# Contiguous first loads with two weight pieces in one pass, a reordered chain of expert choice, and the last row's norm on GpSimd

## What is computed

```python
x = layer_norm(DN_ALPHA * x + hybrid_mixer(x, ...), ln1_g, ln1_b)            # neighbourhood attention ++ short convolution
x = layer_norm(DN_ALPHA * x + memory_cross_attention(x, mem, ...), ln2_g, ln2_b)   # 4 heads over 256 memory rows
x = layer_norm(DN_ALPHA * x + expert_choice_moe(x, ...), ln3_g, ln3_b)

def expert_choice_moe(x, w_router, w_gate, w_up, w_down):                    # 16 experts, hidden width 2048
    affinity = softmax(x @ w_router)                                         # 512 x 16
    gates, idx = lax.top_k(affinity.T, 64)                                   # each expert takes its 64 best tokens
    hid = silu(x[idx] @ w_gate) * (x[idx] @ w_up)
    return scatter_add(idx, (hid @ w_down) * gates)
```

## Time and profile before

| | us |
|---|---|
| median of 3 runs | 1240.74 (1240.32 to 1240.86) |
| profiled execution | 1239.73 |
| its span | 1237.9 |
| PE busy | 1160.5 (94%) |
| DVE busy | 267.6 (22%) |
| ACT busy | 186.7 (15%) |
| POOL busy | 144.1 (12%) |
| chain that ended last | PE 71%, DMA 24%, DVE 2%, ACT 1% |
| HBM read | 440.99 MB |

### The profile page before, as it was taken

One profiled execution on the slowest core, in us unless ns is written; L12 is line 12 of the kernel. 1 busy time (PEld: TensorE's weight loads), 2 busy tenths in 40 slices (PEclk: granted clock), 3 DMA queues, 4 the chain that ended last, 5 costly groups with the idle time before them and its releaser, 6 DMA issues.

```text
span 1237.9 us, 13582 instructions
## 1 busy us (share of the span) xinstructions
PE 1160.5 (94%) x5770; PEld 587.0 (47%) x5770; DVE 267.6 (22%) x510; ACT 186.7 (15%) x341; POOL 144.1 (12%) x71
## 2 busy tenths in 40 slices
PE   8999999999999999999799979987998898899997
PEld 6887778888733433443243324332422342243432
DVE  3022457727700020010002000200010010002025
ACT  4244444143000000010000000000000010000100
POOL 4454334330000300000000000000000000000002
PEclk9999999999999999999999999999998999999999
DMA  9532223249799999999999999999999999999998
GB/s 371 185 135 77 74 94 134 80 186 422 303 338 426 428 423 429 432 431 430 433 428 431 432 432 431 430 434 428 434 431 433 427 436 430 434 426 428 427 427 334
DMA packets 30315, 443.92 MB, mean 359 GB/s; under 512 B 4738, under 2 KB 5122, under 8 KB 10692
## 3 DMA queue, kind: packets, MB, share of 16 engines
q1 hardware_dynamic: 27892, 440.85, 84.7%
q10 hardware_dynamic: 2304, 2.24, 0.5%
q0 software_dynamic: 80, 0.26, 0.1%
HBM read 440.99 MB, written 2.36 MB: 358 GB/s over the span
## 4 chain that ended last, share of the span: by engine, by line
PE 71%; DMA 24%; DVE 2%; ACT 1%; issue 1%; POOL 0%; POOLq 0%; SPq 0%; DVEq 0%; ACTq 0%
DMA ring<-in_w_exp 23%; PE bank L1322 22%; PE bank L1369 14%; PE bank L1196 5%; PE bank L1283 4%; PE bank L837 3%; PE bank L839 3%; PE bank L842 3%; PE bank L1021 1%; PE bank L1023 1%; PE bank L1022 1%; PE bank L1353 1%; PE bank L826 1%; DMA out<-xT 1%; PE bank L977 1%
## 5 line engine op out<-in xcount | busy, mean ns | idle before, releaser
L1322 PE MATMUL bank<-ring,yt 128*64 128x512 f32 x1952 | 440.8, 603 | 41.8 <-DMA ring<-in_w_exp 41.7
L1322 PEld LDWEIGHTS bank<-ring,yt 128*64 128x64 f32 x1952 | 144.0, 139 | 327.0 <-issue 266.8
L1369 PE MATMUL bank<-ring,yt 128*64 128x512 f32 x896 | 203.8, 608 | 20.1 <-DMA ring<-in_w_exp 14.6
L1369 PEld LDWEIGHTS bank<-ring,yt 128*64 128x64 f32 x896 | 64.7, 139 | 138.9 <-issue 123.9
L556 POOL TENSOR_TENSOR stat<-stat 128x1 f32<-128x1 f32 x12 | 18.4, 1530 | 756.7 <-DVE stat L1487 756.7
L1744 DVE TENSOR_TENSOR work<-bank,work 128x512 f32<-128x512 f32 x30 | 20.7, 691 | 355.3 <-PE bank L1322 355.3
L786 ACT ACTIVATE work<-bank 128x512 f32<-128x512 f32 x32 | 19.1, 597 | 478.6 <-PE bank L1322 478.6
L549 POOL TENSOR_TENSOR piece<-ring,piece 128x1024 fp32r<-128x1024 f32 x31 | 74.3, 2397 | 91.3 <-ACT piece L616 91.3
L1760 DVE TENSOR_TENSOR xT<-bank,xT 128x512 f32<-128x512 f32 x56 | 38.7, 692 | 137.1 <-PE bank L1283 137.1
L1196 PE MATMUL bank<-yt,res 128*128 128x128 f32 x512 | 60.0, 275 | 0.0
L1196 PEld LDWEIGHTS bank<-yt,res 128*128 128x128 f32 x512 | 58.4, 192 | 0.8 <-issue 0.8
(11 more groups left out here) (268 smaller groups left out, 1084.3 us busy)
## 6 DMA issues: line engine op xcount, KB each, us to landing
ring<-in_w_exp SPq DMA_DIRECT2D x55, 4096.0 KB, 29.9
ring<-in_w_exp SPq DMA_DIRECT2D x58, 2048.0 KB, 21.4
ring<-in_dense SPq DMA_DIRECT2D x12, 2048.0 KB, 7.8
ring<-in_w_exp SPq DMA_DIRECT2D x5, 3072.0 KB, 27.8
ring<-in_w_exp SPq DMA_DIRECT2D x11, 1024.0 KB, 29.4
spare<-in_w_exp SPq DMA_DIRECT2D x3, 2048.0 KB, 20.0
xT<-in_w_exp SPq DMA_DIRECT2D x4, 1024.0 KB, 9.4
ln<-in_w_exp SPq DMA_DIRECT2D x6, 512.0 KB, 12.8
```

The source lines that it names most:

```text
L1322: mm = nc.tensor.matmul(bank[2 * g + n % 2][64 * c:64 * c + 64, :], xeT[:, kk, 64 * e:64 * e + 64], exp_rhs(at + j, early, k, c), start=kk ...
L1369: mm = nc.tensor.matmul(bank[5][64 * n:64 * n + 64, :], hidT[:, s, 64 * c:64 * c + 64], exp_rhs(at + j, early, s, n), start=(g, c, s) == ( ...
```

## The change

Four things change.

1. The host lays x and the first two pieces of weights out as whole contiguous blocks. SP issues x in four parts with a quarter of pieces 0 and 1 behind each (eight loads instead of five up to there). ACT and POOL handle those quarters of both pieces (four each instead of two), and PE computes both pieces in one pass, with three fillers ahead and a short one in each of the first three steps.
2. DVE adds the two parts of the logits before the turning product (ACT did a copy), so four products and one DVE addition go. The copy of the transposed affinities out of PSUM goes: the rounds read PSUM. The gate copy goes behind the masks. The norm of token tile 3 (`gain` and `shift` on DVE, 128x1024 each) becomes three POOL instructions behind `inverse_std(7)`. The `shift` of token tile 2 is split in halves and put behind the rounds and behind the masks.
3. The rank products take float32r operands, whose constants ACT rounds ahead of the exponential. Two filler products stand behind the transposed masks; one instead of three stands behind the last round of the search.
4. The first gather takes two channel blocks into another bank, then two more; the first expert products start on the first two blocks, and the last four blocks are gathered in the middle of chunk 1 instead of one ahead of chunk 0 and three ahead of chunk 1. The one-hot matrix is made in two halves.

```diff
@@ SP
-            load_x(0)
-            load_first()
-            for m in range(1, KT // 2):
+            for m in range(KT // 2):
                 load_x(m)
-            for m in range(1, 4):
+                load_first(m)
+            for m in range(FIRST_PIECES, 4):
                 load_q(m)
@@ POOL, behind inverse_std(7)
+            row = res[:, TT - 1, :]
+            pool.wait_ge(rstd_ready, 2 * TT)
+            pool.wait_ge(ln_in, 32 * 2)
+            nc.gpsimd.tensor_scalar(row, row, mv_of(TT - 1)[:, 0:1], rstd(TT - 1), ALU.subtract, ALU.mult).then_inc(last_scaled, 1)
+            pool.wait_ge(last_scaled, 1)
+            nc.gpsimd.tensor_tensor(row, row, ln[:, 0, :], ALU.mult).then_inc(gained, 1)
+            pool.wait_ge(gained, 2 * TT)
+            nc.gpsimd.tensor_tensor(row, row, ln[:, 1, :], ALU.add).then_inc(normed, 1)
@@ ACT
-            act.wait_ge(o_logits_done, 1)
-            nc.scalar.activation(o_logits, ps[1][:, :], ACT.Copy).then_inc(o_logits_kept, 1)
+            act.wait_ge(late_in, 16)
+            for to, of in ((tri_r, cst[:, C_TRI:C_TRI + P]), (one_r, cst[:, C_ONE:C_ONE + P]),
+                           (upto_r, late_const(C_UPTO, P)), (below_r, late_const(C_BELOW, P))):
+                nc.scalar.activation(to[:, :], of, ACT.Copy).then_inc(tables_rounded, 1)
@@ PE, first_from_x
                 for k in range(KT):
-                    if k % 4 == 0:
-                        pe.wait_ge(first_hi, k // 4 + 1)
+                    if k % 2 == 0:
+                        pe.wait_ge(first_hi, k // 2 + 1)
                     pe.wait_ge(x_hi_kept, k + 1)
-                    nc.tensor.matmul(pj[0][:, :], hi[:, k, :], x_hi[:, k, :], start=k == 0, stop=False)
+                    for n in range(FIRST_PIECES):
+                        product(n, k, 0, x_hi)
+                    if k < 3:
+                        nc.tensor.matmul(px[0][:, 0:256], kv[:, 0:P], kv[:, 0:256], start=True, stop=True)
                     if k:
                         pe.wait_ge(x_lo_kept, k)
-                        nc.tensor.matmul(pj[0][:, :], hi[:, k - 1, :], x_lo[:, k - 1, :], start=False, stop=False)
+                        for n in range(FIRST_PIECES):
+                            product(n, k - 1, 0, x_lo)
+                    if k % 2 and k > 1:
+                        pe.wait_ge(first_lo, k // 2)
+                        for m in (k - 3, k - 2):
+                            product(0, m, 1, x_hi)
@@ PE, choice
-                keep_clock(3)
+                keep_clock(3 if r < CAP // 8 - 2 else 1)
...
+            keep_clock(2)
+            pe.wait_ge(tables_rounded, 4)
             pe.wait_ge(above_ready, 1)
             pe.wait_ge(turn_kept[TN_MASK % 2], TN_MASK // 2 + 1)
...
-            nc.tensor.matmul(ranks, cst[:, C_TRI:C_TRI + P], mask_tok, start=True, stop=False)
+            nc.tensor.matmul(ranks, tri_r[:, :], mask_r[:, :, :], start=True, stop=False)
@@ PE, pair
-                    gather(0, 4)
-                    gather(4, 5)
+                    gather(0, 2, to=pt, wait_halves=True)
+                    gather(2, 4)
...
-                            if j == 1 and first:
-                                gather(5, 8)
...
+                                if first and j == 1 and k == 2:
+                                    gather(4, 8)
@@ DVE
-            shift(res, 2, TT + 2)
-
-            lg = ps[0][:, 0:TT * E].rearrange("p (t e) -> p t e", t=TT)
+            dve.wait_ge(o_logits_done, 1)
+            for a in range(2):
+                at = slice(256 * a, 256 * a + 256)
+                nc.vector.scalar_tensor_tensor(o_logits[:, at], x1_logits[:, at], ALPHA, ps[1][:, at], ALU.mult, ALU.add)\
+                    .then_inc(o_logits_kept, 1)
...
-            nc.vector.tensor_copy(gate.rearrange("p i t e -> p t i e"), aff.rearrange("p t (i e) -> p t i e", e=2))\
-                .then_inc(gate_kept, 1)
-
-            gain(res, TT - 1, 2 * TT - 1)
             link(nc.vector.memset(lists[:, 0:1], 2.0))
             dve.wait_ge(turned, TN_AFF + 1)
-            nc.vector.tensor_copy(afft, pt[TN_AFF % 2][halves, 0:256]).then_inc(turn_kept[TN_AFF % 2], 1)
-            dve.wait_ge(turn_kept[TN_AFF % 2], TN_AFF // 2 + 1)
+            afft = pt[TN_AFF % 2][halves, 0:256]
...
+            shift_half(TT - 2, 0).then_inc(last_shifted, 1)
...
-            shift(res, TT - 1, 2 * TT - 1)
+            dve.wait_ge(last_shifted, 1)
+            shift_half(TT - 2, 1).then_inc(normed, 1)
+            nc.vector.tensor_copy(gate.rearrange("p i t e -> p t i e"), aff.rearrange("p t (i e) -> p t i e", e=2))\
+                .then_inc(gate_kept, 1)
```

More of the change, by code:

```diff
@@ L138 @@
 LAST_PARTS = {CPP - 2: 2, CPP - 1: 4}
-START_FILLERS = 2
+START_FILLERS = 3
+FIRST_PIECES = 2
+FIRST_LOADS = KT // 2
 def build(nc, x, x_turned, mem_turned, dense, na_bias, conv_w, ln1_g, ln1_b,
@@ L241, in build @@
         col_sums = stat[:, 64:96]
-        sum_groups = [cst[:, C_SUM + n * E:C_SUM + n * E + E] for n in range(2)]
+        sum_groups = cst[:, C_SUM:C_SUM + E]
         router_sums = stat[:, 64:96].rearrange("p (a e) -> p a e", a=2)
@@ L533, in _ @@
             nc.gpsimd.memset(neg_half, -0.5).then_inc(half_set, 1)
-            for a in range(2):
-                k = slice(4 * a, 4 * a + 4)
-                pool.wait_ge(first_hi, a + 1)
-                nc.gpsimd.tensor_tensor(piece[:, 0, 1, k, :], raw_piece(0)[:, k, :], piece[:, 0, 0, k, :].bitcast(F32),
+            for g in range(FIRST_LOADS):
+                pool.wait_ge(first_hi, g + 1)
+                nc.gpsimd.tensor_tensor(first_part(g, 1), first_raw(g), first_part(g, 0).bitcast(F32),
                                         ALU.subtract).then_inc(first_lo, 1)
@@ L629, in split_x, with split_first @@
                 nc.scalar.activation(x_hi[:, k, :], x_raw[:, k, :], ACT.Copy).then_inc(x_hi_kept, 1)
-            def split_first(a):
-                k = slice(4 * a, 4 * a + 4)
-                act.wait_ge(first_in, 16)
-                nc.scalar.activation(piece[:, 0, 0, k, :], raw_piece(0)[:, k, :], ACT.Copy).then_inc(first_hi, 1)
-            split_x(0)
-            split_first(0)
-            for k in range(1, 4):
-                split_x(k)
-            split_first(1)
-            for k in range(4, KT):
-                split_x(k)
-            split(1)
+            def split_first(g):
+                act.wait_ge(first_in[g], 16)
+                nc.scalar.activation(first_part(g, 0), first_raw(g), ACT.Copy).then_inc(first_hi, 1)
+            for g in range(FIRST_LOADS):
+                split_x(2 * g)
+                split_first(g)
+                split_x(2 * g + 1)
             nc.scalar.activation(edge_x[0].rearrange("p k (s t) -> p k s t", s=2), edge_tokens(x_raw), ACT.Copy)                .then_inc(edge_hi_kept, 1)
@@ L896, in _ @@
             first_from_x()
-            for p in range(1, 8):
+            for p in range(FIRST_PIECES, 8):
                 from_x(p)
@@ L1177, in _ @@
             keep_clock(5)
-            pe.wait_ge(chosen_ready, 1)
-            turn(TN_MASK, [(chosen[:, a, P * b:P * b + P], 2 * E, P) for a in range(2) for b in range(2)])
+            pe.wait_ge(turn_kept[TN_MASK % 2], TN_MASK // 2)
+            for a, ready in enumerate((gt_ready, chosen_ready)):
+                pe.wait_ge(ready, 1)
+                for b in range(2):
+                    at = P * (2 * a + b)
+                    mm = nc.tensor.transpose(pt[TN_MASK % 2][:, at:at + 2 * E], chosen[:, a, P * b:P * b + P], ident[halves, halves])
+            mm.then_inc(turned, 1)
+            keep_clock(2)
+            pe.wait_ge(tables_rounded, 4)
             pe.wait_ge(above_ready, 1)
@@ L1320, in pair @@
                                 kk = 4 * (n // 2) + k
+                                if first and j == 0 and k == 2:
+                                    pe.wait_ge(xe_kept, 1)
+                                if first and j == 1 and k == 2:
+                                    gather(4, 8)
                                 for c in range(2):
@@ L1839, in dense_chunks @@
               by_row(w_o), by_row(w_o.T)]
+    first, rest = chunks[0][:, 0:FIRST_PIECES], chunks[0][:, FIRST_PIECES:]
+    first = first.reshape(P, FIRST_PIECES, FIRST_LOADS, 2, P).transpose(2, 0, 1, 3, 4)
+    chunks[0] = np.concatenate([first.reshape(-1), rest.transpose(1, 0, 2, 3).reshape(-1)])
     return np.stack([c.reshape(P, SLOT) for c in chunks])
@@ L1860 @@
         "x": by_column(np.asarray(inputs["x"])[0]),
-        "x_turned": by_row(by_column(np.asarray(inputs["x"])[0]).T),
+        "x_turned": by_row(by_column(np.asarray(inputs["x"])[0]).T).reshape(P, KT // 2, 2, S).transpose(1, 0, 2, 3),
         "na_bias": bias_table(np.asarray(inputs["na_rpb"])[0]),
```

173 lines of the change are left out of this document (106 added, 67 removed).

## The result

The changed kernel takes 1234.39 us (median of 4 runs, 1233.03 to 1236.2), the kernel before 1240.8 beside it: a ratio of 0.9948, 95% interval 0.9935 to 0.996, some 6.4 us less. Two later sets of runs, on other chips, gave 5.6 and 5.4 us less. The prediction, 1243.7 with a range from 1235.8, had the wrong sign. What came was its first rival, "the chain gets shorter" (1236.1), and a little more. The profiled execution is the slowest of the four, 1236.2 us with a span of 1234.4, only 3.5 us under the span before: its work up to the last stores runs 4.65 us ahead, and these took 10.20 us where they had 9.08.

A forecast was written before the change was run, and what follows sets the result against it. It took the DMA plateau, started by pair 0, to bound the kernel. Start -1.3, softmax +6.1, behind it -0.9 and order in pair 0 -0.9 gave +3.0 on 1240.74: 1243.7 us, range 1235.8 to 1246.2.

The forecast's parts named there:

- first rival: Softmax: POOL's three instructions leave DVE's small steps alone, affinities 0.2 us earlier; 1236.1 us in all, chance 0.20.
- The frame: DMA queue: the end is the plateau's start plus fixed bytes, so moving pair 0's start moves the end equally.
- Nothing arrives: DMA queue: its backlog, not pair 0, sets the plateau, so no term counts; 1240.7 us, chance 0.05.
- Softmax, +6.1: Choice of experts: POOL's three instructions hold DVE's two-SBUF-operand softmax steps; +6.1 us (+3.9 to +6.8).
- That rival: Softmax: TENSOR_SCALAR does not block, only the division is caught, affinities +1.9 us; 1238.2 us, chance 0.08.
- Idle PE, low clock and piled-up fillers (+1.2): Behind the softmax: PE idles 6 us; slower transposes cost 0.2 us, fillers of the rounds +1.0 (0 to 2.0).
- MAX8 behind the affinities: Behind the softmax: without gate copy, gain and PSUM copy only the transpose is left, 0.6 us: -1.3.
- Ranks: Behind the softmax: eight float32r rank products take one pass each, 1.25 us in all: -0.85 (0 to -1.1).
- The half pick: Between ranks and gather: six fillers stand as before, so the earlier half of `pick` gains nothing.
- Order in pair 0: First expert pair: chunk 0 starts 0.9 us earlier and reloads move forward; -0.9 us (-1.2 to 0).
- Start, -1.3: Kernel start: the third piece starts near 19.75 instead of 21.05 us; -1.3 us (-2.0 to -0.1).
- the 0.8 for the clock: Kernel start: half-speed products before TensorE reaches 2.4 GHz cost 0.8 us within the sum of 19.6.

The follow-up runs named there:

- e3: The kernel before with only the new start (contiguous first blocks, one pass over two pieces, new fillers): 1238.34 us, ratio 0.9984.
- e1: The changed kernel with POOL's TENSOR_SCALAR on row 3 made as two TENSOR_TENSORs, same arithmetic: 1241.11 us, ratio 1.0001 to the kernel before.
- e6: The changed kernel with POOL's TENSOR_SCALAR doing only the subtraction, the multiplication left out: 1235.51 us, 4.8 under the kernel before.
- e12: The changed kernel unaltered, run once more beside other runs of its set: 1234.81 us, 5.4 under the kernel before.
- e7: The changed kernel with the eight rank products read as float32 in place of float32r: 1236.0 us, 4.3 under the kernel before.
- e8: The changed kernel with the first pair's pick and gather in the order of the kernel before: 1235.17 us, 5.1 under the kernel before.

## Why the prediction was wrong

**The frame held.** The plateau has its old level, and what moved the start of pair 0 moved the end: 1.9 us in e3 all the way through, 6.2 us at e1's gather as 6.5 in the time. Below 1 us it can't be followed: e6 and e12, whose first reloads are 0.17 us apart, are 4.6 and 6.2 us ahead in arrived bytes. "Nothing arrives" is refuted.

**Softmax, +6.1: the step that failed.** The prediction concluded from the earlier trace rows that a DVE instruction with two SBUF operands waits until "POOL's instruction is over, however small it is". "However small" is right (e1, 128x64). "POOL's instruction" is wrong: all the rows had a TENSOR_TENSOR on POOL, and the first of the three here is a TENSOR_SCALAR, which lets the small steps pass: the term of +6.1 measured -0.3 (the last step 2.11 us earlier, 1.82 of it from the start). The prediction had noticed that no row was a witness for it, gave the case 0.08, and let the blanket rule of the Trainium skill, "SBUF — State Buffer", section "SBUF: two separate sides" (a lock against any GpSimd instruction that reads SBUF) stand as the likelier. Here the measurement differs from the page: POOL's TENSOR_SCALAR reads `res` in SBUF, and four two-operand steps beside it take 0.22 to 0.23 us. With TENSOR_TENSORs the prediction's price was nearly right, though for a row of three instructions where e1 has four, two of them shorter: 9.55 us from POOL's start to the affinities by its working, 8.80 measured in e1.

**And a second size in the same step.** That rival still had the last step caught, +1.9, since it took 2.7 us for the TENSOR_SCALAR from an instruction with one operation. With two it takes 3.81, and covers the softmax to its end. So the first rival comes nearest to the time and the second has the mechanism.

**What hung on it.** Idle PE, low clock and piled-up fillers (+1.2) fell away with it. In e1 they can be seen: PE idles 5.72 us ahead of the transpose, the granted clock is 0.50 from 321 to 327 and 1.00 by 328, when two rounds are left. The transposes came 0.2 us later as priced, but from last MAX8 to the read of the ranks it took 0.3 us more, not 1.0.

**Terms that held.** MAX8 behind the affinities: -1.3 predicted, -1.37 measured. Between first MAX8 and first rank product: -0.16 measured (10.17 before, 10.01 now). Ranks: -0.85 against -0.93, and 1.0 in e7. The half pick gains nothing behind six fillers: the gather starts 1.33 us behind DVE's read, before and after. Order in pair 0: -0.9 against -0.99 at the first reload; how much of it reaches the end, e8 leaves open (0.55 in the medians, whose runs overlap).

**Start, -1.3: too small.** Measured -1.9 (trace) and -2.1 (e3). The sum runs on from the first product without a wait, but in the trace PE waits for data until 9.23, and from there only 42 products and a filler are left. From 5.42 to 9.23 it has 2.2 us of work and 1.6 us of waiting, which no term stood for. That the first product came at 5.42, not 6.6 (ACT is through with the first quarter at 5.37, and the fillers reach the higher clock at 4.82), gains nothing by itself; the 0.8 for the clock was not lost; and only one of the three fillers, 0.44 of 1.3 us, is behind the wait.

## What to carry to other kernels

A row that shows one engine holding another is a witness for that kind of instruction with that kind of operand, not for the engine: before a general rule is priced, look which operation stands in each row, and give the case without a witness a chance that can decide the sign. When work is moved beside a chain, order it so that an instruction that does not hold (here POOL's TENSOR_SCALAR) lies beside the chain's small two-operand steps and the ones that do lie beside steps with one operand or PSUM; how long it covers is part of the design, here 0.97 us of margin. Fillers that keep a clock belong only where the engine would wait anyway, and behind the last arrival each is paid in full.
